# The fourth block's product ahead of the down chunk in the first pair of a chain, and the last norm from the accumulator, in a four-layer decoder trunk

## The chip, the cores and the metric

One NeuronCore of one Trainium2 chip runs the whole program. The metric is the device time of one execution in microseconds (us), given as the median of several runs; weights lie in HBM when it begins and are streamed in once. All arithmetic is float32. To get its precision from TensorE every weight chunk is split in two float32r parts (w_hi, w_lo), every activation likewise, and each product is made of three.

## What is computed

Four layers, each a half-step SwiGLU, an attention (stick-breaking, differential, forgetting, stick-breaking) and a second half-step SwiGLU, for 256 tokens of width 1024; at the end one more RMSNorm.

```python
D_MODEL, SEQ, DEPTH, D_FF, HEAD_DIM, EPS = 1024, 256, 4, 2816, 128, 1e-6

def rms_norm(x, g):
    y = x * rsqrt(mean(x * x, -1) + EPS)
    return y * g

def swiglu(x, w_gate, w_up, w_down):
    return (silu(x @ w_gate) * (x @ w_up)) @ w_down

for i in range(DEPTH):
    x = x + 0.5 * swiglu(rms_norm(x, norm_g[i, 0]), ffn_w_gate[i, 0], ffn_w_up[i, 0], ffn_w_down[i, 0])
    h = rms_norm(x, norm_g[i, 1])
    ...
    x = x + mix @ w_o[i]
    x = x + 0.5 * swiglu(rms_norm(x, norm_g[i, 2]), ffn_w_gate[i, 1], ffn_w_up[i, 1], ffn_w_down[i, 1])
return rms_norm(x, final_g)
```

## The kernel before

**Chunks.** The weights are worked through as 424 chunks of 128x2048 (1 MB each), in the order in which TensorE uses them. A DMA brings each into one of five slots of `raw` (or one of the two of `extra`), ScalarE copies it to `w_hi` (`hi`, L535), VectorE subtracts to `w_lo` (`lo`, L919), and TensorE multiplies; `w_hi` and `w_lo` are rings of six. `split_to(c)` on ScalarE and on VectorE takes all chunks up to c; where those calls stand among the other work sets the order of both engines. SP's queue issues the loads in the order of the list that `plan()` makes; each waits until its slot has been read (by `lo`, or by a form), and those behind it wait too.

**Units.** An FFN has 11 units of 256 hidden columns. A plain unit needs the chunks top and bottom (24 products of 128x512 each) and, when its hidden values are known, down (24 more, into the four banks of `acc`). Units 2 and 3, 4 and 5, 7 and 8, 9 and 10 are taken in pairs (`SEVEN` = 2, 4, 7, 9): a pair is a two by two block product (token halves by column blocks), made with seven products of 12 (`quarter`) in place of eight. Their chunks are b11, b21, b22 and the sums t1, t2, t3, t4. t1 is added up by DMAs (GpSimd's `first_weight_sums`); t3 = b22 + b12, t2 = t3 + b11 and t4 = b21 + t2 are *forms*, made by VectorE in place (`form`, L931, L935, L939). On the token side the sums are S1 to S4 (`token_sums_lo`, L1011). The four results are blocks c11, c21 (the first unit) and c12, c22 (the second): sums on VectorE (`sum_12` L1068, `sum_22` L1074), silu on ScalarE (c11 L618, c21 L623, c12 L629, c22 L636) and the gate product on VectorE (c11 L1078, c21 L1084, c12 L1090, c22 L1097). `pair_hidden` (L1687) transposes them on TensorE, `hidden_hi` (L558) and `hidden_lo` (L979) split them, and `unit_down` (L1493 to L1495 into acc) uses them.

**First and second of a chain.** Pair 4 follows pair 2, and 9 follows 7, with no plain unit between: 4 and 9 are *chained*. For a first pair (2 or 7) `pair_order` gives TensorE and the chunk list the order b11, t1, t2, b21, t3, down of the unit ahead, t4, b22. The transposes of its c11 and c21 stand behind the next pair's b11, and its own down chunk two products later. b11 of a t1 sum is loaded into slot `SUMS`, b22 into slot `EXTRA`, both of the tensor `extra`, which hold one pair at a time: b22 of a chained pair may be loaded when `lo` has taken b22 of the pair ahead of it.

**Around a norm.** `mean` (L961) is made by VectorE from sums of squares, GpSimd raises it to the power -1/2 (`r_col`, L499, L500). In the differential layer the last head pair's output product is kept apart (`output_apart`) and scaled afterwards: `mean_apart` (L1263), `r_apart` (L503, L504), `update` (L1385), with three `early_update`s (L1377) of the rest ahead of `mean_apart`; TensorE then turns x (L1537). At the end of the program ScalarE copies each bank of `acc`, which holds 2x, to x (`update`, L821), squares it (L830), and VectorE and ScalarE scale by `r_col` and `final_gain` (L1473, L1481, L890) into four stores.

## Time and profile before

| | us |
|---|---|
| median of 3 runs | 1882.12 (1881.24 to 1883.84) |
| the profiled execution | 1877.97 |
| its span, first to last instruction | 1876.2 |
| TensorE's products busy | 1853.3 (99%) |
| VectorE busy | 1562.6 (83%) |
| ScalarE busy | 1166.9 (62%) |
| granted clock of TensorE, mean | 0.999 |

Busy times are sums over instructions in one profiled execution. TensorE's products overlap each other in it, and their ends are modelled, so the idle time that the profile shows ahead of a product is less than the distance from start to start would give. The eight FFNs take about 177 us each, the four attentions about 110. All times of a row count from the start of the span.

### The profile page before, as it was taken

Reading aid. Unit: us, or ns where it says so; the run is one execution under the profiler, and the core shown is the slowest. Engines: PE = TensorE matmul, PEld = TensorE weight load, DVE = VectorE, ACT = ScalarE, POOL = GpSimd, SP = SyncE. Lnnn points to the kernel's source line nnn. Section 1 sums busy time; section 2 is a strip of 40 time slices with the busy share of each in tenths; the row PEclk is TensorE's granted clock in tenths of the full one; section 3 lists DMA queues with packets and bytes.
Section 4 is the critical chain, followed back from the end, with each engine's and each line's share of the span. In section 5 each row is a group of like instructions: output and inputs, shape, how many; then the busy total and the mean of one; then the engine's idle time right before and its main releaser. Section 6 shows DMA issues by size and latency. Waiting matters only on the chain.

```text
span 1876.2 us, 22732 instructions
## 1 busy us (share of the span) xinstructions
PE 1853.3 (99%) x9268; PEld 1566.1 (83%) x9268; DVE 1562.6 (83%) x1295; ACT 1166.9 (62%) x1220; POOL 60.3 (3%) x75
## 2 busy tenths in 40 slices
PE   9999999999999999999999999999999999999998
PEld 7788898888878899788888888987888888998886
DVE  7979568989888969998988995788898898569896
ACT  6666456666656645666665674465667567556665
POOL 1000000000000000100000000010000000001000
PEclk9999999999999999999999999999999999999999
DMA  8775445776677543577667763467775766437762
GB/s 300 261 290 226 180 157 180 226 289 264 200 249 272 235 151 134 183 254 286 266 187 272 255 247 121 149 227 245 270 278 190 274 221 246 157 108 252 277 238 79
DMA packets 59272, 417.28 MB, mean 222 GB/s; under 512 B 7192, under 2 KB 7456, under 8 KB 8992
## 3 DMA queue, kind: packets, MB, share of 16 engines
q1 hardware_dynamic: 53968, 380.09, 51.8%
q0 software_dynamic: 4608, 33.56, 9.5%
q10 hardware_dynamic: 592, 2.17, 0.3%
q8 instruction: 74, 1.21, 0.2%
q14 instruction: 30, 0.25, 0.0%
HBM read 414.74 MB, written 1.06 MB: 222 GB/s over the span
## 4 chain that ended last, share of the span: by engine, by line
PE 80%; DVE 12%; DMA 4%; ACT 2%; issue 2%; POOL 0%; SPq 0%; POOLq 0%; DVEq 0%; ACTq 0%
PE work L1493 16%; PE work L1495 16%; PE work L1494 16%; PE acc L1493 9%; PE acc L1495 9%; PE acc L1494 9%; DVE w_lo L919 6%; DMA extra<-stream_dram 3%; DMA raw<-stream_dram 1%; PE work L1687 1%; DVE raw L935 1%; PE acc L1537 1%; DVE raw L931 1%; PE work L1865 1%; PE work L1729 0%
## 5 line engine op out<-in xcount | busy, mean ns | idle before, releaser
L919 DVE TENSOR_TENSOR w_lo<-raw,w_hi 128x2048 fp32r<-128x2048 f32 x359 | 810.3, 2284 | 14.2 <-ACT w_hi L535 14.0
L535 ACT ACTIVATE w_hi<-raw 128x2048 fp32r<-128x2048 f32 x359 | 677.1, 1910 | 128.7 <-DVE raw L935 76.2
L1493 PE MATMUL work<-w_hi,xg 128*128 128x512 f32 x880 | 346.6, 394 | 1.1 <-DVE w_lo L919 1.1
L1495 PE MATMUL work<-w_hi,xg 128*128 128x512 f32 x880 | 343.5, 390 | 0.0
L1494 PE MATMUL work<-w_lo,xg 128*128 128x512 f32 x880 | 343.0, 390 | 0.0
L1493 PE MATMUL acc<-w_hi,m_hi 128*128 128x512 f32 x824 | 328.3, 398 | 6.3 <-DVE w_lo L919 6.1
L1495 PE MATMUL acc<-w_hi,m_lo 128*128 128x512 f32 x824 | 321.8, 391 | 0.0
L1494 PE MATMUL acc<-w_lo,m_hi 128*128 128x512 f32 x824 | 321.2, 390 | 0.0
L1495 PE MATMUL work<-w_hi,wide_r 128*128 128x512 f32 x512 | 199.8, 390 | 0.0
L1493 PEld LDWEIGHTS work<-w_hi,xg 128*128 128x128 f32 x880 | 165.4, 188 | 34.9 <-DVE w_lo L919 1.7
L1495 PEld LDWEIGHTS work<-w_hi,xg 128*128 128x128 f32 x880 | 165.3, 188 | 34.8
L1494 PEld LDWEIGHTS work<-w_lo,xg 128*128 128x128 f32 x880 | 165.5, 188 | 33.0
L1493 PEld LDWEIGHTS acc<-w_hi,m_hi 128*128 128x128 f32 x824 | 154.9, 188 | 38.1 <-DVE w_lo L919 8.4
L1495 PEld LDWEIGHTS acc<-w_hi,m_lo 128*128 128x128 f32 x824 | 154.7, 188 | 32.9
L1494 PEld LDWEIGHTS acc<-w_lo,m_hi 128*128 128x128 f32 x824 | 155.1, 188 | 30.0
L1493 PE MATMUL work<-xg,w_hi 128*128 128x256 f32 x512 | 148.9, 291 | 0.2
L919 DVE TENSOR_TENSOR w_lo<-extra,w_hi 128x2048 fp32r<-128x2048 f32 x64 | 146.2, 2284 | 0.0
L1494 PE MATMUL work<-xg,w_hi 128*128 128x256 f32 x512 | 145.0, 283 | 0.0
L1495 PE MATMUL work<-xg,w_lo 128*128 128x256 f32 x512 | 145.0, 283 | 0.0
L535 ACT ACTIVATE w_hi<-extra 128x2048 fp32r<-128x2048 f32 x64 | 122.3, 1911 | 4.4 <-DMA extra<-stream_dram 4.4
L1495 PEld LDWEIGHTS work<-w_hi,wide_r 128*128 128x128 f32 x512 | 96.1, 188 | 20.4
L1493 PE MATMUL work<-w_hi,scratch_r 128*128 128x512 f32 x256 | 103.1, 403 | 1.2 <-DVE w_lo L919 1.2
(211 smaller groups left out, 2324.8 us busy)
## 6 DMA issues: line engine op xcount, KB each, us to landing
raw<-stream_dram SPq DMA_DIRECT2D x295, 1024.0 KB, 7.3
extra<-stream_dram SPq DMA_DIRECT2D x64, 1024.0 KB, 4.9
extra<-stream_dram POOLq DMA_DIRECT2D x32, 1024.0 KB, 8.0
x<-x_dram SPq DMA_DIRECT2D x2, 512.0 KB, 8.2
raw<-stream_dram ACTq DMA_DIRECT2D x2, 512.0 KB, 8.0
scratch<-cum_rows ACTq DMA_DIRECT2D x1, 1024.0 KB, 6.5
cst<-consts_dram SPq DMA_DIRECT2D x1, 832.0 KB, 6.4
out_dram<-x SPq DMA_DIRECT2D x3, 256.0 KB, 2.5
```

Of the source, the lines that this page charges most:

```text
L535: nc.scalar.activation(w_hi[:, c % RING, :], raw_at(place), ACT.Copy).then_inc(hi_ready, 1)
L919: nc.vector.tensor_tensor(w_lo[:, c % RING, :], raw_at(place), w_hi[:, c % RING, :].bitcast(F32), ALU.subtract).then_inc(lo_ready, 1)
L931: ins = nc.vector.tensor_tensor(t3, b22, t3, ALU.add)
L935: ins = nc.vector.tensor_tensor(t2, t3, t2, ALU.add)
L1493: nc.tensor.matmul(dst, a_hi, b_hi, start=start, stop=False, skip_group_check=skip)
L1494: nc.tensor.matmul(dst, a_hi, b_lo, start=False, stop=False, skip_group_check=skip)
L1495: return nc.tensor.matmul(dst, a_lo, b_hi, start=False, stop=stop, skip_group_check=skip)
L1537: ins = nc.tensor.matmul(turned(bank)[:, d, :], x_part(bank)[:, d * P:(d + 1) * P], ident, is_transpose=True, start=d == 0, stop=d == FIRS ...
L1687: ins = nc.tensor.transpose(hidden_bank(s)[:, t * T + tb * P:t * T + (tb + 1) * P], h[:, t * P:(t + 1) * P], ident)
L1865: nc.tensor.matmul(bank, v[:, 0, cols], w[:, 0:T], start=True, stop=True)
```

## The change

Five pieces.

1. In a first pair b22's chunk and product stand ahead of the down chunk and of t4: b11, t1, t2, b21, t3, b22, down, t4 (`pair_order`, TensorE's `pair_step`).
2. The other engines follow: the blocks are now done in the order c11, c22, c12, c21 for every pair (`block_count`), with VectorE's sum and gate for c12 and ScalarE's silu for c12 earlier, and VectorE's forms of t3 and t2 of the chained pair behind gate c21.
3. `plan()` puts the load of a chained pair's b22 ahead of the load of its b21 (it was behind that of the down chunk). It still waits for `lo` of the b22 ahead.
4. From the second FFN on, `hidden_lo(0)` stands behind the third token sum's low part and the form of t3. At the end of the differential layer VectorE takes one more chunk's low part ahead of `mean_apart`, and the three early updates come behind it; ScalarE takes one chunk's high part earlier.
5. At the end of the program the four copies of `acc` to x are gone: squares, gains and outputs read `acc` itself, 2x, and the mean is taken with 4 EPS.

```diff
@@ pair_order
-    return [("b11", s), ("t1", s), ("t2", s), ("b21", s), ("t3", s), ("down", s - 1), ("t4", s), ("b22", s)]
+    return [("b11", s), ("t1", s), ("t2", s), ("b21", s), ("t3", s), ("b22", s), ("down", s - 1), ("t4", s)]
@@ plan
+            if what == "t4" and j in SEVEN[:-1] and not chained(following(j)):
+                loads.append(("b22", layer, n % 3, following(j), EXTRA, ("lo", c0 + order.index(("b22", j)) + 1)))
+            if what == "b21" and chained(j):
+                loads.append(("b22", layer, n % 3, j, EXTRA, ("lo", c0 + order.index(("b22", j - 2)) + 1)))
...
-            if what == "down" and chained(j + 2):
-                loads.append(("b22", layer, n % 3, j + 2, EXTRA, ("lo", c0 + order.index(("b22", j)) + 1)))
...
@@ ScalarE, pair_step
                     split_to(q + 8)
                     silu_22()
+                    split_to(q + 9)
+                    silu_12()
                     split_to(q + 10)
                     silu_21()
                     split_to(q + 11)
-                    silu_12()
@@ ScalarE, end of an attention
                     if j:
                         weights(b)
+                    if j == PAIRS and kind == DIFF:
+                        split_to(c0 + ATT_CHUNKS + 1)
@@ ScalarE, last norm
-                        update(n, i)
-                        square_sum(n, i)
+                        last_square_sum(i)
...
+            def last_square_sum(i):
+
+                n, bank = NORMS - 1, banks_of(NORMS - 1)[i]
+                act.wait_ge(acc_ready, BANKS * (n - 1) + i + 1)
+                act.wait_ge(squares_ready, BANKS * n + i - 1)
+                nc.scalar.activation(squares[i % 2], acc[:, bank, :], ACT.Square, scale=D ** -0.5,
                                      accum_out=sums[:, bank // TB, bank % TB:bank % TB + 1]).then_inc(squares_ready, 1)
@@ VectorE, plain_step
-                    if s == 1:
+                    if s == 1 and n:
+                        token_sums_lo((0, 1, 2))
+                    elif s == 1:
                         token_sums_lo((0, 1))
                         hidden_lo(0)
                         token_sums_lo((2,))
...
                     form("t3", q)
+                    if s == 1 and n:
+                        hidden_lo(0)
@@ VectorE, first_of_chain
                         if s == SEVEN[0]:
                             hidden_lo(s - 1)
-                        split_to(q + 5)
-                        if s == SEVEN[0]:
                             token_sums_lo((3,))
                         split_to(q + 6)
                         gate_11()
                         sum_22()
                         split_to(q + 7)
+                        sum_12()
                         split_to(q + 8)
                         gate_22()
-                        split_to(q + 9)
+                        gate_12()
+                        split_to(q + 10)
+                        gate_21()
                         form("t3", q + 8)
-                        gate_21()
-                        sum_12()
-                        split_to(q + 10)
                         form("t2", q + 8)
-                        gate_12()
                         hidden_lo(s)
@@ VectorE, end of the differential attention
                         apart_split(b)
+                        split_to(c0 + ATT_CHUNKS + 1)
+                        apart_mean()
                         for i in range(BANKS - 1):
                             early_update(i)
-                        apart_mean()
-                        split_to(c0 + ATT_CHUNKS + 1)
@@ VectorE, last norm
                     final_output(0, 0)
+                    final_mean(1)
                     final_gained()
-                    final_mean(1)
...
-                part = x_part(TB * half + tb)
-                nc.vector.scalar_tensor_tensor(out=part, in0=part, scalar=r_col[:, tb:tb + 1],
+                bank = TB * half + tb
+                nc.vector.scalar_tensor_tensor(out=x_part(bank), in0=acc[:, bank, :], scalar=r_col[:, tb:tb + 1],
@@ TensorE, pair_step of a first pair
                     quarter(chain, sum_of(S3), at["t3"], False, False)
+                    if s == SEVEN[0]:
+                        pe.wait_ge(token_lo_ready, BANKS * (f + 1))
+                    quarter(3, sum_of(S4), at["b22"], False, True)
                     unit_down(s - 1).then_inc(down_used, 1)
                     pe.wait_ge(pair_sums_ready, 2 * p + sum_count("c22"))
                     quarter(chain, block_of(1, 1), at["t4"], False, True)
-                    if s == SEVEN[0]:
-                        pe.wait_ge(token_lo_ready, BANKS * (f + 1))
-                    quarter(3, sum_of(S4), at["b22"], False, True)
```

What stands on VectorE in a row, in the first pair (unit 2) of the third FFN, before (line numbers of the kernel before; those of the changed kernel are 10 to 14 higher). `w_lo<-extra` is b22 where it follows the sum, and t1 where it precedes the form of t3 (L931):

```order
L1011 TENSOR_TENSOR wide_r<-wide,wide_r 128x512
L919 TENSOR_TENSOR w_lo<-raw,w_hi 128x2048
L1078 SCALAR_TENSOR_TENSOR scratch<-work,r_col,scratch 128x256
L1074 TENSOR_TENSOR scratch<-work,scratch 128x512
L919 TENSOR_TENSOR w_lo<-extra,w_hi 128x2048
L919 TENSOR_TENSOR w_lo<-raw,w_hi 128x2048
L1097 SCALAR_TENSOR_TENSOR scratch<-scratch,r_neg 128x256
L919 TENSOR_TENSOR w_lo<-extra,w_hi 128x2048
L931 TENSOR_TENSOR raw<-extra,raw 128x2048
L1084 SCALAR_TENSOR_TENSOR pair_h<-work,r_col,pair_h 128x256
L1068 TENSOR_TENSOR scratch<-work,scratch 128x512
L919 TENSOR_TENSOR w_lo<-raw,w_hi 128x2048
```

The same stretch of VectorE in the changed kernel:

```order
L1021 TENSOR_TENSOR wide_r<-wide,wide_r 128x512
L929 TENSOR_TENSOR w_lo<-extra,w_hi 128x2048
L929 TENSOR_TENSOR w_lo<-raw,w_hi 128x2048
L1092 SCALAR_TENSOR_TENSOR scratch<-work,r_col,scratch 128x256
L1088 TENSOR_TENSOR scratch<-work,scratch 128x512
L929 TENSOR_TENSOR w_lo<-raw,w_hi 128x2048
L1082 TENSOR_TENSOR scratch<-work,scratch 128x512
L929 TENSOR_TENSOR w_lo<-raw,w_hi 128x2048
L1111 SCALAR_TENSOR_TENSOR scratch<-scratch,r_neg 128x256
L1104 SCALAR_TENSOR_TENSOR scratch<-scratch,r_neg 128x256
L929 TENSOR_TENSOR w_lo<-extra,w_hi 128x2048
L929 TENSOR_TENSOR w_lo<-raw,w_hi 128x2048
```

b22's low part (the first `w_lo<-extra`) moved from behind the sum for c22 to the front, with the sum and the gate for c12 (L1082, L1104) up as well; gate c21 (L1098) and then the form of t3 follow behind the last row.

SP's queue around the loads of the chained pair 4 of the third FFN, before; `extra` alone is b11 for the sum t1 or b22, the rest goes to `raw`:

```order
L454 DMA raw<-stream_dram 128x2048 x8
L454 DMA extra<-stream_dram 128x2048
L454 DMA raw<-stream_dram 128x2048 x4
L454 DMA extra<-stream_dram 128x2048
L454 DMA raw<-stream_dram 128x2048
L454 DMA extra<-stream_dram 128x2048
```

And in the changed kernel:

```order
L454 DMA raw<-stream_dram 128x2048 x8
L454 DMA extra<-stream_dram 128x2048
L454 DMA raw<-stream_dram 128x2048 x2
L454 DMA extra<-stream_dram 128x2048
L454 DMA raw<-stream_dram 128x2048 x3
L454 DMA extra<-stream_dram 128x2048
```

The load of b22 (the second `extra`) went from behind b11, b12, b21 and down 2 to behind b11 and b12.

VectorE at the end of the differential layer, before:

```order
L919 TENSOR_TENSOR w_lo<-raw,w_hi 128x2048 x2
L1255 SCALAR_TENSOR_TENSOR m_lo<-work,subln_s,m_hi 128x256 x2
L1377 TENSOR_TENSOR x<-acc,x 128x512 x3
L1263 TENSOR_SCALAR mean_apart<-work 128x2
L919 TENSOR_TENSOR w_lo<-raw,w_hi 128x2048
L1385 SCALAR_TENSOR_TENSOR x<-work,r_apart,x 128x512 x2
```

And in the changed kernel:

```order
L929 TENSOR_TENSOR w_lo<-raw,w_hi 128x2048 x2
L1266 SCALAR_TENSOR_TENSOR m_lo<-work,subln_s,m_hi 128x256 x2
L929 TENSOR_TENSOR w_lo<-raw,w_hi 128x2048
L1274 TENSOR_SCALAR mean_apart<-work 128x2
L1388 TENSOR_TENSOR x<-acc,x 128x512 x3
L1396 SCALAR_TENSOR_TENSOR x<-work,r_apart,x 128x512 x2
```

The chunk's low part and the three early updates have changed places around `mean_apart`, for which GpSimd waits.

## Rows read from the trace of the kernel before

**Rows 1.** The page's first section: busy time, share of the span, instructions.

```profile
PE 1853.3 (99%) x9268; PEld 1566.1 (83%) x9268; DVE 1562.6 (83%) x1295; ACT 1166.9 (62%) x1220; POOL 60.3 (3%) x75
```

**Rows 2.** Timeline of TensorE, last FFN, start of down 2; start, length, engine, line.

```profile
1756.10 0.39 PE L1495 MATMUL work<-w_hi,xg 128*128 128x512 f32 x1
1756.33 0.60 PE L1687 MATMUL work<-cst,scratch 128*128 128x128 f32 x4
1756.68 0.48 PE L1493 MATMUL acc<-w_hi,m_hi 128*128 128x512 f32 x1
```

**Rows 3.** Waits of TensorE, 110 to 1870 us: total, times, longest.

```profile
PE acc L1493 <- DVE w_lo L919: 4.7, 5, 1.4
...
PE work L1687 <- DVE pair_h L1084: 0.4, 1, 0.4
```

**Rows 4.** Waits of TensorE, 60 to 90 us (first FFN).

```profile
PE work L1687 <- DVE pair_h L1084: 1.6, 1, 1.6
PE acc L1493 <- DVE w_lo L919: 1.4, 1, 1.4
```

**Rows 5.** Timeline of TensorE, third FFN, start of down 2.

```profile
542.09 0.60 PE L1687 MATMUL work<-cst,scratch 128*128 128x128 f32 x4
544.06 0.50 PE L1493 MATMUL acc<-w_hi,m_hi 128*128 128x512 f32 x1 [1.38 <-DVE w_lo L919]
```

**Rows 6.** Timeline of VectorE, third FFN, first pair; in brackets idle time and releaser.

```profile
519.03 2.29 DVE L919 TENSOR_TENSOR w_lo<-raw,w_hi 128x2048 fp32r<-128x2048 f32 x1 [0.35 <-ACT w_hi L535]
...
522.71 2.28 DVE L919 TENSOR_TENSOR w_lo<-extra,w_hi 128x2048 fp32r<-128x2048 f32 x1
...
533.12 2.29 DVE L931 TENSOR_TENSOR raw<-extra,raw 128x2048 f32<-128x2048 f32 x1 [3.33 <-DMA extra<-stream_dram]
...
541.72 4.49 DVE L919 TENSOR_TENSOR w_lo<-raw,w_hi 128x2048 fp32r<-128x2048 f32 x2
```

**Rows 7.** The loads of L454 issued from 514 to 531 us.

```profile
DMA to landing us min/median/max: 7.1/8.1/10.2
```

**Rows 8.** Windows: busy time of each engine, TensorE's clock, DMA share, GB/s.

```profile
530.00:535.00 5.00, 5.00 (x24) 4.15 (x23) 1.88 (x1) 2.28 (x2) 0.00 (x0) 1.00 0.99 359
```

**Rows 9.** Timeline of ScalarE, silu of c21 in the third FFN, unit 2.

```profile
530.19 0.47 ACT L623 ACTIVATE pair_h<-work,r_col 128x256 f32<-128x256 f32 x1 [2.57 <-PE work L1495]
```

**Rows 10.** Timeline of VectorE, first FFN, form of t3 for unit 4.

```profile
69.05 2.29 DVE L931 TENSOR_TENSOR raw<-extra,raw 128x2048 f32<-128x2048 f32 x1 [1.88 <-DMA extra<-stream_dram]
```

**Rows 11.** Timeline of VectorE, third FFN, low part of unit 0's h.

```profile
497.67 0.69 DVE L979 TENSOR_TENSOR m_lo<-work,m_hi 128x512 fp32r<-128x512 f32 x1 [2.97 <-ACT m_hi L558]
```

**Rows 12.** Timeline of VectorE, end of the differential layer.

```profile
758.96 1.87 DVE L1377 TENSOR_TENSOR x<-acc,x 128x512 f32<-128x512 f32 x3
761.63 0.16 DVE L1263 TENSOR_SCALAR mean_apart<-work 128x2 f32<-128x2 f32 x1 [0.80 <-PE work L1900]
761.71 2.28 DVE L919 TENSOR_TENSOR w_lo<-raw,w_hi 128x2048 fp32r<-128x2048 f32 x1
765.11 1.41 DVE L1385 SCALAR_TENSOR_TENSOR x<-work,r_apart,x 128x512 f32<-128x512 f32 x2 [1.12 <-POOL r_apart L504]
```

**Rows 13.** Timeline of GpSimd, the same place.

```profile
761.87 2.53 POOL L503 TENSOR_TENSOR r_apart<-mean_apart,half_neg 128x1 f32<-128x1 f32 x1 [97.48 <-DVE mean_apart L1263]
764.37 0.54 POOL L504 TENSOR_TENSOR r_apart<-mean_apart,half_neg 128x1 f32<-128x1 f32 x1
```

**Rows 14.** Timeline of GpSimd, end of the program.

```profile
1868.02 0.56 POOL L512 TENSOR_TENSOR r_col<-mean,half_neg 128x1 f32<-128x1 f32 x1 [63.73 <-DVE mean L1464]
1870.73 1.00 POOL L512 TENSOR_TENSOR r_col<-mean,half_neg 128x1 f32<-128x1 f32 x1 [2.15 <-DVE mean L1464]
```

**Rows 15.** Timeline of TensorE, first turn of x behind the differential layer.

```profile
765.92 0.55 PE L1537 MATMUL acc<-cst,x 128*128 128x128 f32 x3 [1.49 <-DVE x L1385]
```

**Rows 16.** Timeline of ScalarE, the last bank at the end of the program.

```profile
1869.11 0.60 ACT L821 ACTIVATE x<-acc 128x512 f32<-128x512 f32 x1
1869.74 0.63 ACT L830 ACTIVATE wide<-x 128x512 f32<-128x512 f32 x1
```

More of the change, by code:

```diff
@@ L85, in part_count, with block_count @@
     return [part for part, unit in pair_order(s) if unit == s].index(what) + 1
-def block_count(s, which):
-    return (("c11", "c22", "c12", "c21") if chained(s) else ("c11", "c22", "c21", "c12")).index(which) + 1
+def block_count(which):
+    return ("c11", "c22", "c12", "c21").index(which) + 1
 def sum_count(which):
@@ L184, in plan @@
                 loads.append((load, layer + 1, 0, SEVEN[0], place, ("lo", c0 + order.index((last, SEVEN[-1])) + 1)))
-            if what == "down" and chained(j + 2):
-                loads.append(("b22", layer, n % 3, j + 2, EXTRA, ("lo", c0 + order.index(("b22", j)) + 1)))
             if what == "down" and j + 1 in SEVEN[:-1]:
                 loads.append(("b11", layer, n % 3, following(j + 1), SUMS, ("lo", c0 + order.index(("t1", j + 1)) + 1)))
-            if what == "t4" and j in SEVEN[:-1] and not chained(following(j)):
-                loads.append(("b22", layer, n % 3, following(j), EXTRA, ("lo", c0 + order.index(("b22", j)) + 1)))
     return uses, loads
@@ L603, in seeded @@
                         if chained(s):
-                            act.wait_ge(pair_h_ready, 4 * (p - 1) + block_count(s - 2, "c21"))
+                            act.wait_ge(pair_h_ready, 4 * (p - 1) + block_count("c21"))
                         nc.scalar.activation(work[:, seed_bank(s), :], work[:, chain_bank(s), :],
@@ L830, in square_sum @@
                 nc.scalar.activation(squares[i % 2], x_part(bank), ACT.Square, scale=D ** -0.5,
+                                     accum_out=sums[:, bank // TB, bank % TB:bank % TB + 1]).then_inc(squares_ready, 1)
+            def last_square_sum(i):
[3 more added lines that the diff above has]
+                nc.scalar.activation(squares[i % 2], acc[:, bank, :], ACT.Square, scale=D ** -0.5,
                                      accum_out=sums[:, bank // TB, bank % TB:bank % TB + 1]).then_inc(squares_ready, 1)
@@ L1076, in gate_11 @@
                     def gate_11():
-                        dve.wait_ge(pair_silu_ready, 4 * p + block_count(s, "c11"))
+                        dve.wait_ge(pair_silu_ready, 4 * p + block_count("c11"))
                         nc.vector.scalar_tensor_tensor(out=first_part[:, 0:COLS], in0=work[:, seed_bank(s), COLS:2 * COLS],
@@ L1082, in gate_21 @@
                     def gate_21():
-                        dve.wait_ge(pair_silu_ready, 4 * p + block_count(s, "c21"))
+                        dve.wait_ge(pair_silu_ready, 4 * p + block_count("c21"))
                         nc.vector.scalar_tensor_tensor(out=pair_h[:], in0=work[:, chain_bank(s), COLS:2 * COLS],
@@ L1088, in gate_12 @@
                     def gate_12():
-                        dve.wait_ge(pair_silu_ready, 4 * p + block_count(s, "c12"))
+                        dve.wait_ge(pair_silu_ready, 4 * p + block_count("c12"))
                         nc.vector.scalar_tensor_tensor(out=first_sum[:, 0:COLS], in0=first_sum[:, COLS:2 * COLS],
@@ L1094, in gate_22 @@
                     def gate_22():
-                        dve.wait_ge(pair_silu_ready, 4 * p + block_count(s, "c22"))
+                        dve.wait_ge(pair_silu_ready, 4 * p + block_count("c22"))
                         place = fifth_copy(s)
@@ L1463, in final_mean @@
                 dve.wait_ge(squares_ready, BANKS * (NORMS - 1) + 2 * tb + 2)
-                nc.vector.scalar_tensor_tensor(out=mean[:, tb:tb + 1], in0=sums[:, 0, tb:tb + 1], scalar=EPS,
+                nc.vector.scalar_tensor_tensor(out=mean[:, tb:tb + 1], in0=sums[:, 0, tb:tb + 1], scalar=4 * EPS,
                                                in1=sums[:, 1, tb:tb + 1], op0=ALU.add,
@@ L1477, in final_gained @@
             def final_gained():
[L1479 removed]
+                dve.wait_ge(squares_ready, BANKS * NORMS)
                 dve.wait_ge(final_loaded, 16)
[L1481 removed]
+                nc.vector.tensor_tensor(last_gained, acc[:, 3, :], final_gain[:, HALF_D:], ALU.mult).then_inc(last_gained_ready, 1)
             dve.wait_ge(gain_loaded, 16)
@@ L1630, in pair_step @@
                     if chained(s):
-                        pe.wait_ge(pair_h_ready, 4 * (p - 1) + block_count(s - 2, "c11"))
+                        pe.wait_ge(pair_h_ready, 4 * (p - 1) + block_count("c11"))
                         quarter(chain, block_of(0, 0), at["b11"], True, False)
@@ L1682, in pair_hidden @@
                     for block in ("c12", "c22") if second else ("c11", "c21"):
-                        pe.wait_ge(pair_h_ready, 4 * p + block_count(first, block))
+                        pe.wait_ge(pair_h_ready, 4 * p + block_count(block))
                     for t in range(2):
@@ L1701, in plain_step @@
                         pe.wait_ge(lo_ready, c + 1)
-                        pe.wait_ge(pair_h_ready, 4 * p + block_count(s - 2, "c11"))
+                        pe.wait_ge(pair_h_ready, 4 * p + block_count("c11"))
                         gate_up(s, 0, c, top)
-                        pe.wait_ge(pair_h_ready, 4 * p + block_count(s - 2, "c21"))
+                        pe.wait_ge(pair_h_ready, 4 * p + block_count("c21"))
                         gate_up(s, 1, c, top).then_inc(top_used, 1)
```

2 lines of the change are left out of this document (removed).

## The prediction

> **What bounds the kernel now.** The page's first section comes first: TensorE has work for 1853.3 of 1876.2 us [rows 1], and its products follow each other every 0.23 us (1756.10 to 1756.33, [rows 2]). The change removes no product. So only two kinds of time can be won: gaps between products, and the ends. The view of TensorE's waits lists the gaps: from 110 us on five waits of a down product for VectorE's w_lo, 4.7 us in all, and one of 0.4 us for pair_h [rows 3]; one more of 1.5 us is for x, and comes in part 2; in the first FFN 1.6 us for pair_h and 1.4 us for w_lo [rows 4]. The idle time shown is less than the gap, because a product's modelled end overlaps the next one. With no wait a down product begins 0.35 us after the transposes ahead of it begin (1756.33 to 1756.68, [rows 2]); in the third FFN it is 1.97 us (542.09 to 544.06, [rows 5]), a gap of 1.62 where 1.38 is shown. I add 0.24 to each.
>
> Why is VectorE late there? Its timeline [rows 6] shows chunk after chunk, 2.20 us apart (two of 2.28 take 4.49 at 541.72), then 3.33 us idle ahead of the form of t3 for the second unit pair (533.12), released by the DMA into extra. Then 2.20 us steps again, so that the low part of down 2 is begun at 541.72 and done at 544.0, when the product of 544.06 begins. The load waited for is b22 of the next pair. It may overwrite extra only when VectorE has taken the low part of the present b22 (522.71 to 524.9); loads issued in this stretch take 7.1 to 10.2 us, median 8.1 [rows 7], with the DMA engines 0.99 busy [rows 8]: 525.0 plus 8.1 is 533.1. The cause is when the slot comes free.
>
> **Part 1, fourth block first.** In each of 16 first pairs (two for each of 8 FFNs) b22's product, its high and low parts and with them the release of extra go ahead of the down chunk and t4. No instruction is added or removed. In the third FFN I go along VectorE's new order with the old steps. The low part of the down chunk still begins at 519.03, since it waits for ScalarE's high part, which stands behind a copy of t2's sum. b22's low part lies ahead of it, so it ends by 519.0 instead of 524.9; with 8.1 us its load lands at 527, with the slowest of [rows 7] at 529.2. After 519.03: gate c11 and the sum for c22 as now, t4 at 522.7 to 524.9, the sum for c12 (0.6) to 525.5, b11 of the next pair to 527.7, two gates of 0.4 to 528.5, t1 and b21 to 532.9. Now gate c21 needs t4's product. Now TensorE is through with t4 at 530.0, and ScalarE begins its silu 0.2 us later and takes 0.47 (530.19, [rows 9]). With b22's 12 products (2.7 us) ahead of it t4 ends at 532.7: the silu runs from 532.9 to 533.4, the gate to 533.8. Then the forms of t3 and t2 (the load is there) to 538.2, a low part of h 0.6, and down 2's low part to 541.0, where it was 544.0. TensorE arrives: b11 (2.7) ends at 535.4, its transposes need c21, there since 533.8, **margin 1.6 us**; with 0.35, t1, b21 and 0.35 more it is at down 2 at 541.6, **margin 0.6 us**. Both gaps of this FFN close. The second first pair of each FFN (unit 7) has no gap now, and by the same steps gets none.
>
> The sum from 110 us on: 4.7 + 5 x 0.24 = 5.9, and 0.5 for the wait at 536 (0.36 idle there, and the overlap): **6.4 us**. The lower bound: the margin at down 2 is missed by 0.6 us in each of the five FFNs with such a wait, 3.0 us less: 3.4.
>
> In the first FFN VectorE waits 1.88 us for the same load (69.05, [rows 10]) and is behind from the start, so the gaps don't close: they move with its chain, which loses the 1.88 and gains about 0.1 of waiting for t4. The gap at the plain unit behind it hangs on loads issued behind the same chain and moves along. I take **1.8 us**; bounds 0.9 (b22 now stands behind a low part of the token sums, and TensorE can wait for it, up to half of the gain) and 3.3 (both waits of [rows 4] whole).
>
> Costed at nothing: from the second FFN on the first low part of h goes behind the third token sum and the form of t3, which is 0.6 + 2.2 = 2.8 us of work put into an idle time of 2.97 us (497.67, [rows 11]); if b12's load were late there, the first down product would wait behind the form. ScalarE's silu of c12 ahead of c21 stands while t4 is still running. On SP's queue b22's load now stands ahead of b21's and down 2's, and everything behind it waits for that release: b21's goes out by 519.4 instead of 515.7 and is needed as a low part at 530.7; down 2's goes out at 524.9 instead of 521.3 and is needed at 538.8. GpSimd's own loads (the adding ones) keep their release.
>
> **Part 2, end of the differential layer.** VectorE takes the next chunk's low part ahead of mean_apart, and three early updates behind it. mean_apart waited 0.8 us for TensorE's squares (761.63) anyway, so it starts as before. What follows differs: now a 2.28 us w_lo runs beside GpSimd's power (761.71, [rows 12]), which takes 2.53 us, and a second one 0.54 [rows 13]; with nothing beside it one takes 0.56 (1868.02, [rows 14]). x is ready for its update at 764.9, VectorE starts at 765.11, TensorE at 765.92 after 1.49 us idle [rows 15]. After the change three updates of 0.6 run there (to 763.5), with one operand in PSUM. No row shows a power beside such. Free it ends at 761.87 + 0.56 + 0.54 = 763.0, and the update starts when VectorE is through, 763.5: 1.5 us won. Held until 763.5 it ends at 764.5, the update begins at 764.6: 0.5 won. I take **1.5**, the row of 0.56 being nearest as long as one operand is not in SBUF; bounds 0.5 and 1.6.
>
> The Trainium skill, SBUF — State Buffer, Who interferes with whom, says that a VectorE instruction with two SBUF inputs blocks a GpSimd instruction that reads SBUF, one with at most one doesn't. By that rule, which the 2.53 beside a w_lo bears out, it is 1.5; were updates blocking too it would be 0.5.
>
> **Part 3, last norm from the accumulator.** Four copies of 0.6 leave ScalarE. Its last chain is a copy at 1869.11, which PSUM's last bank releases, and then the square at 1869.74 [rows 16]; without the copy the square starts 0.6 us sooner. A square out of PSUM has no row; a copy out of it took 0.60, the square 0.63 from SBUF, so 0.6 to 0.7. The last power (1.00 us, beside a VectorE step with two SBUF inputs, 1870.73, [rows 14]) may fall to 0.56, but VectorE then has the last three outputs to make in a row, as now. The end moves by **0.6 us**; bounds 0.3 and 0.9.
>
> **The sum.** 6.4 + 1.8 + 1.5 + 0.6 = 10.3 us. Against the profiled execution (1877.97 us, 1876.2 of it span) that is 1867.7. The three runs' median, 1882.12, lies 4.1 us above it; the same step gives **1871.8 us**. All lower bounds: 3.4 + 0.9 + 0.5 + 0.3 = 5.1, 1877.0. All upper ones: 6.7 + 3.3 + 1.6 + 0.9 = 12.5, 1869.6. Runs of one kernel differ by 2.6 us, so about 0.2% (3.8 us) can be told from no change.
>
> **Rivals.** *Down 2 stays late.* The idle time on VectorE goes, but its chain has only 0.6 us to spare; one more wait of 1.2 us, say for ScalarE, and each of five FFNs keeps 0.6: 7.3 us won, 1874.8. For: the margin; against: the last FFN, where VectorE has hardly a DMA wait and TensorE's product follows after 0.35 [rows 2].
>
> *The load in front only swaps places.* The DMA engines are 0.99 busy [rows 8], and b21's 1 MB now runs behind b22's. If it landed after 531 ScalarE's queue, and behind it silu c21, would be late; at 533 the gain of part 1 from 110 us on is gone and only 3.9 us are left: 1878.2, at the edge of no change. Against: by 519.4 plus 10.2 it lands by 529.6. The Trainium skill, DMA: Bandwidth & Descriptors, Two DMAs through the same engine are not ordered, says that in one queue of an engine descriptors start in order; by it b21's really stands behind, and the landing would be as I took it.
>
> *Slower: c21 ends last.* t4's form comes 2.7 us later on TensorE, and between it and the transposes of c11 and c21 stands one product of 2.7 us instead of two. The price starts when gate c21 is more than 1.6 us later than I reckon, at all 16 pairs, also at the eight of unit 7 that have no gap. At 2.6 us late: 16 x 1.0 lost, part 1 not won, parts 2 and 3 won: 1882.1 + 16 - 2.1 = 1896. Against: VectorE has nothing between b21's low part and the gate.
>
> *The change doesn't do what it says*: the release is not sooner because high parts are held by TensorE's progress. Then parts 2 and 3 alone are left, 2.1 us: 1880.0. Against: b22's high part needs only a ring place freed six chunks before.
>
> **Chances.** The forecast 0.58 (1869.6 to 1874); down 2 partly late 0.22; swapped places or no earlier release 0.12 (one half of it within 0.2%); c21 last, slower 0.05; more won than all upper bounds 0.03. The range 1868.5 to 1878 leaves out the slow case, half of the third, and little else. Faster by over 0.2% (below 1878.4) 0.86; within 0.2% 0.09; slower 0.05.
>
> **What the changed profile would show.** VectorE's form of t3 in unit 4 without a DMA wait in all eight FFNs; TensorE's waits from 110 us on without the w_lo row of a down product, and pair_h without waits; r_apart's first power near 0.6 us, x's wait under 0.3; ScalarE's last square ending near 0.8 us after TensorE's last product. Wrong would be: waits of TensorE for pair_h at many pairs, or of ScalarE for the DMA of b21 past 531 in the third FFN.

## The result, and the profile after

| | before | after |
|---|---|---|
| median (lowest to highest), runs side by side, us | 1881.24 (1874.98 to 1883.84), 5 runs | 1866.98 (1866.62 to 1867.86), 5 runs |
| the profiled execution, us | 1877.97 | 1866.62 |
| its span, us | 1876.2 | 1864.8 |

The ratio is 0.9926, with a 95% interval of 0.991 to 0.9942: 14.3 us less by the medians, 11.4 by the spans of the two profiles. The forecast was 10.3 for a profile, and 1871.8 us with 1868.5 to 1878.0 around it for the median. The direction and the change of the profile were foreseen; the time itself lies 1.5 us below the range.

Two more things stand in the table. Before's runs lie 8.9 us apart, those of the changed kernel 1.2. And before's median lies 3.3 us above its own profiled execution, after's 0.4. Both have the same cause, and the experiments found it.

The page of the changed kernel: the busy times, then the chain that ended last, by engine (TensorE's part of it was 80% before, VectorE's 12%).

```profile
PE 1851.8 (99%) x9268; PEld 1566.0 (84%) x9268; DVE 1562.9 (84%) x1295; ACT 1164.8 (62%) x1216; POOL 58.0 (3%) x75
...
PE 89%; DVE 5%; DMA 2%; ACT 1%; issue 1%; SPq 0%; DVEq 0%; ACTq 0%
```

TensorE's work is what it was [rows 1]; ScalarE has 1216 instructions, four less than before: the copies. TensorE's waits from 110 to 1870 us, which answer [rows 3] (total, times, longest), are these two and no other:

```profile
PE work L1504 <- DVE m_lo L1266: 0.5, 1, 0.5
PE work L1845 <- DVE k_t L1226: 0.3, 1, 0.3
```

The row of w_lo (4.7 us), the one of pair_h and the one of x are gone. VectorE in the third FFN, which answers [rows 6]; the brackets hold idle time and releaser:

```profile
512.24 2.28 DVE L929 TENSOR_TENSOR w_lo<-extra,w_hi 128x2048 fp32r<-128x2048 f32 x1
...
530.80 0.48 DVE L1098 SCALAR_TENSOR_TENSOR pair_h<-work,r_col,pair_h 128x256 f32<-128x256 f32 x1 [0.43 <-ACT pair_h L623]
531.21 2.28 DVE L941 TENSOR_TENSOR raw<-extra,raw 128x2048 f32<-128x2048 f32 x1
533.52 2.29 DVE L945 TENSOR_TENSOR raw<-raw 128x2048 f32<-128x2048 f32 x1
535.73 0.69 DVE L989 TENSOR_TENSOR m_lo<-work,m_hi 128x512 fp32r<-128x512 f32 x1
536.33 4.49 DVE L929 TENSOR_TENSOR w_lo<-raw,w_hi 128x2048 fp32r<-128x2048 f32 x2
```

b22's low part stands at 512.24, the gate of c21 at 530.80 with 0.43 us of waiting for its silu, and the form of t3 at 531.21 with no bracket: it waits for nothing. TensorE at the same place, transposes and then down 2, beside [rows 5]:

```profile
538.75 0.60 PE L1698 MATMUL work<-cst,scratch 128*128 128x128 f32 x4
539.11 0.47 PE L1504 MATMUL acc<-w_hi,m_hi 128*128 128x512 f32 x1
```

0.36 us from the one to the other, where it was 1.97. The end of the differential layer, GpSimd and then TensorE's first turn of x, beside [rows 13] and [rows 15]:

```profile
756.83 0.55 POOL L503 TENSOR_TENSOR r_apart<-mean_apart,half_neg 128x1 f32<-128x1 f32 x1 [97.45 <-DVE mean_apart L1274]
757.34 0.55 POOL L504 TENSOR_TENSOR r_apart<-mean_apart,half_neg 128x1 f32<-128x1 f32 x1
```

```profile
759.27 0.64 PE L1548 MATMUL acc<-cst,x 128*128 128x128 f32 x4
```

The first power takes 0.55 us where it took 2.53, and x's wait of 1.49 is gone.

**Where the 11.4 us went.** The same products are compared at their starts in the two profiles. Near 110 us, before and after:

```profile
111.47 0.27 PE L1687 MATMUL work<-cst,scratch 128*128 128x128 f32 x1
```

```profile
109.47 0.27 PE L1698 MATMUL work<-cst,scratch 128*128 128x128 f32 x1
```

| product | before | after | earlier by |
|---|---|---|---|
| transposes behind the first FFN's last pairs | 111.47 | 109.47 | 2.0 |
| third FFN, transposes ahead of down 2 | 542.09 | 538.75 | 3.3 |
| third FFN, down 2 | 544.06 | 539.11 | 5.0 |
| first turn of x behind the differential layer | 765.92 | 759.27 | 6.7 |
| last product | 1868.68 | 1857.83 | 10.9 |
| end of the span | 1876.2 | 1864.8 | 11.4 |

Of the 6.7 at x, 1.6 come between the power (761.87 before, 756.83 after: 5.0) and the turn of x. So the first FFN gave 2.0 (forecast 1.8), the pairs behind it 10.9 - 2.0 - 1.6 = 7.3 (6.4), the differential layer 1.6 (1.5), the end 0.5 (0.6).

In the first FFN the two gaps of [rows 4] have become smaller (0.2 and 0.7 us where they were 1.6 and 1.4), and a new one stands ahead of b22's product, which the forecast had named as possible:

```profile
56.92 0.47 PE L1504 MATMUL work<-w_hi,wide_r 128*128 128x512 f32 x1 [0.75 <-DVE w_lo L929]
```

### The profile page after: what moved, and what is told of

Read it like the earlier page. It is cut to its first block, busy times and chain, and to the rows that moved or that the text cites. A ratio compares the mean times of both kernels' runs of the same rounds, so it can differ in the third digit from the quotient of the medians.

```text
span 1864.8 us, 22728 instructions
## 1 busy us (share of the span) xinstructions
PE 1851.8 (99%) x9268; PEld 1566.0 (84%) x9268; DVE 1562.9 (84%) x1295; ACT 1164.8 (62%) x1216; POOL 58.0 (3%) x75
## 4 chain that ended last, share of the span: by engine, by line
PE 89%; DVE 5%; DMA 2%; ACT 1%; issue 1%; SPq 0%; DVEq 0%; ACTq 0%
PE work L1504 18%; PE work L1506 18%; PE work L1505 18%; PE acc L1506 10%; PE acc L1504 10%; PE acc L1505 10%; DVE w_lo L929 3%; DMA raw<-stream_dram 2%; PE work L1698 1%; PE acc L1548 1%; ACT w_hi L535 1%; PE work L1876 1%; PE work L1740 1%; PE work L1842 0%; PE work L1846 0%
```

## The experiments

They ask three things. First, which part brings what, and is the distance between before's median and its profile something that stays or something that the change removes? Second, if it is VectorE's wait for one load that makes TensorE's gaps, what closes them: the earlier release of extra, or the new order? Third, what are the small parts worth, and is anything left? Three theories run through the expectations. **A**: the gaps come from VectorE's wait for b22's load ahead of the form of t3, and the length of that load differs from execution to execution. **B**: the new order of products and low parts closes them whatever the load does. **C**: the early release is what counts. In the expectations of the next group "Rival B" is something else: before's median lies above its profile by an offset of the chip or the session that has nothing to do with the waits.

### One part at a time

The kernel before, unchanged, run once more:

> The kernel before, unchanged, profiled once more. The first profile (span 1876.2 us) was of an execution 4 us below the median of the runs. Theory A (TensorE's waits in this kernel hang on how long a load takes, and that differs from execution to execution): this profile shows waits for w_lo and pair_h that differ from the first by up to a few us, and the span goes with them; the runs spread over 3 us or more. Rival B (an offset of a chip or a session that has nothing to do with the waits): the waits are those of the first profile within 0.5 us in sum, whatever the span.

Part 1 alone (pieces 1 to 3 of the change, and nothing of pieces 4 and 5):

> Part 1 alone: fourth block first, with the order of ScalarE, VectorE and the loads that goes with it; without the moved low part of unit 0's h, without the change at the differential layer and in the last norm. Prediction's steps: 6.4 + 1.8 = 8.2 us off the span of the profiled execution of before (1868.0). Theory A: against the runs of before on the same chip about 12 us, with a spread of 1 us. Rival B: 8.2 us against them. In the profile: no wait of TensorE for w_lo of a down product from 110 us on; x still waits 1.5 us.

The end of the differential layer alone, on ScalarE and then on VectorE:

```diff
                     if j:
                         weights(b)
+                    if j == PAIRS and kind == DIFF:
+                        split_to(c0 + ATT_CHUNKS + 1)
...
                         apart_split(b)
+                        split_to(c0 + ATT_CHUNKS + 1)
+                        apart_mean()
                         for i in range(BANKS - 1):
                             early_update(i)
-                        apart_mean()
-                        split_to(c0 + ATT_CHUNKS + 1)
```

> The end of the differential layer alone: one low part ahead of mean_apart, the three early updates behind it, one high part earlier on ScalarE. Forecast: the first power of r_apart falls from 2.53 to 0.56 us, TensorE's wait for x from 1.5 us to under 0.3; 1.5 us in all, which the runs can't tell from no change. If an update with one operand in PSUM holds GpSimd as well, the power takes 1.7 us or more and 0.5 us are won. Theory A: spread and median of the runs otherwise as before.

The last norm from the accumulator alone:

> The last norm from the accumulator alone. Forecast: from the end of the last product to the end of the span 0.6 us less than in before (there 7.1 us), the last power 0.56 us in place of 1.00; in the runs no change that can be told.

| kernel | runs | median (lowest to highest), us | ratio to before (95%) | span of its profile |
|---|---|---|---|---|
| before, in the same session | 25 | 1879.62 (1874.05 to 1883.52) | | |
| before once more | 10 | 1880.13 (1877.21 to 1881.94) | 0.9999 (0.999 to 1.0008) | 1875.4 |
| part 1 | 4 | 1868.82 (1868.43 to 1869.23) | 0.9942 (0.9926 to 0.9959) | 1866.8 |
| differential layer | 10 | 1876.73 (1873.17 to 1881.68) | 0.9986 (0.9976 to 0.9997) | 1875.3 |
| last norm | 10 | 1877.83 (1874.59 to 1882.89) | 0.9997 (0.9985 to 1.001) | 1880.5 |

Part 1 by itself takes 10.8 us from the median, and the spread with it: 0.8 us between its runs, where the kernels without it have 4.7 to 9.5. Parts 2 and 3 are hardly told from nothing on that ground, though their profiles show them: with part 2 the first power takes 0.55 us and the wait for x is gone, with part 3 the span ends 7.0 us behind the start of the last product (1873.52 to 1880.5), where it was 7.5. What differs between executions is in the waits. VectorE's waits for this load from 110 to 1880 us, first before (TensorE's wait for w_lo beside it is in [rows 3], 4.7 us):

```profile
DVE raw L931 <- DMA extra<-stream_dram: 13.9, 9, 3.3
```

Before once more, TensorE's waits for w_lo and VectorE's for the load:

```profile
PE acc L1493 <- DVE w_lo L919: 4.4, 5, 1.3
...
DVE raw L931 <- DMA extra<-stream_dram: 12.6, 8, 2.6
```

The same two of the kernel with the last norm alone, whose profile is 4.3 us longer than before's:

```profile
PE acc L1500 <- DVE w_lo L926: 8.5, 7, 1.4
...
DVE raw L938 <- DMA extra<-stream_dram: 19.4, 9, 3.4
```

The last of these executions waited 5.5 us longer on VectorE than before's, 3.8 us longer on TensorE, and lasted 4.3 us longer in spite of its shorter end. Between the two executions of the kernel before the difference is small, 0.7 us in TensorE's waits for w_lo and pair_h and 0.8 in the span, so that pair alone would hardly decide against the offset; this third profile does. Which FFNs wait differs too, and at which pair: at unit 9 the form of t3 mostly waits 0.1 us, but 1.94 in the first FFN of before once more and 1.24 in the fourth of the kernel with the last norm alone. In the third one before has 3.33 us [rows 6]; in the other execution of the same kernel the form stands right behind the low part:

```profile
528.81 2.28 DVE L919 TENSOR_TENSOR w_lo<-extra,w_hi 128x2048 fp32r<-128x2048 f32 x1
531.14 2.29 DVE L931 TENSOR_TENSOR raw<-extra,raw 128x2048 f32<-128x2048 f32 x1
```

The loads around it say why: issues and landing times of before, 520 to 528 us, b22's issued at 525.0 and landing about 8 us later:

```profile
L454 SPq DMA_DIRECT2D extra<-stream_dram x1: 328/328/328, 525.0 to 525.0; - x1
...
DMA to landing us min/median/max: 7.1/8.0/10.2
```

The same loads in before once more; b22's is the shortest of the three, and was there when VectorE came:

```profile
L454 SPq DMA_DIRECT2D extra<-stream_dram x1: 328/328/328, 526.3 to 526.3; - x1
...
DMA to landing us min/median/max: 4.7/5.8/8.1
```

And the windows (the last two columns are the DMA engines' busy share and GB/s), first before, where the stretch of [rows 8] follows, then before once more:

```profile
520.00:525.00 5.00, 5.00 (x23) 4.13 (x22) 4.61 (x5) 5.00 (x5) 0.00 (x0) 1.00 0.92 354
525.00:530.00 5.00, 5.00 (x24) 4.14 (x23) 4.79 (x3) 2.13 (x2) 0.00 (x0) 1.00 0.98 356
```

```profile
520.00:525.00 5.00, 5.00 (x24) 4.14 (x23) 4.28 (x4) 5.00 (x6) 0.00 (x0) 1.00 1.01 403
525.00:530.00 5.00, 5.00 (x24) 4.14 (x23) 5.00 (x4) 3.32 (x2) 0.00 (x0) 1.00 0.96 370
530.00:535.00 5.00, 5.00 (x24) 4.14 (x23) 4.50 (x5) 2.28 (x2) 0.00 (x0) 1.00 1.02 416
```

At about the same busy share (0.92 to 0.99, and 0.96 to 1.02) the DMA engines moved 354 to 359 GB/s in the one execution and 370 to 416 in the other. The kernel before turned such differences into time, and the changed one doesn't.

The sessions of the experiments, each on another chip, differ in the same way: before's medians were 1879.62, 1881.54 and 1876.92 us in them, while the three kernels that have part 1's gain and nothing else (part 1 itself, and below the load made short and the form placed later) measured 1868.82, 1868.76 and 1868.6, one in each. So a chip or a session does have its part in before's median, but not as an offset outside the waits, as rival B had it: with the waits it goes.

### The load made short, with the old order

```diff
-                sp.dma_start(raw_at(place), stream[i]).then_inc(done[place] if place in done else raw_loaded[place], 16)
+                cols = CHUNK // 16 if LOADS[i][0] == "b22" and chained(LOADS[i][3]) else CHUNK
+                sp.dma_start(raw_at(place)[:, 0:cols], stream[i][:, 0:cols]).then_inc(
+                    done[place] if place in done else raw_loaded[place], 16)
```

> The kernel before, in which the load of a chained pair's b22 moves only the first 128 of its 2048 columns (the rest of that weight block is left out of the computation; every instruction of the engines stays). Nothing of the changed order is in it. Theory A (TensorE's gaps come from VectorE's wait for this load, and its length, 4.7 to 8.1 us in the profiles so far, differs from execution to execution): no form of t3 in unit 4 waits for a DMA, the gain of part 1 is there with the old order, 1868 to 1872 us, and the runs lie within 1 us of each other, where before's lie within 9. Rival B (the new order of products and low parts itself closes the gaps): 1876 to 1880 us, gaps and spread as before.

Measured: 1868.76 us (1868.59 to 1869.07, 4 runs), before beside it 1881.54 (1877.92 to 1885.56, 7 runs), ratio 0.993 (0.9914 to 0.9947). That is part 1's time and part 1's spread without anything of part 1. VectorE in the third FFN still waits a little, since the small load is queued behind others, but 0.72 us don't reach TensorE:

```profile
524.30 2.28 DVE L921 TENSOR_TENSOR w_lo<-extra,w_hi 128x2048 fp32r<-128x2048 f32 x1
527.30 2.29 DVE L933 TENSOR_TENSOR raw<-extra,raw 128x2048 f32<-128x2048 f32 x1 [0.72 <-DMA extra<-stream_dram]
```

Theory B falls as far as it says that the new order is needed; A stands. One thing is left open here: the edit also takes 16 times 15/16 of a megabyte off the DMA engines, which may make other loads shorter. The form placed later, below, gets the same time with every load whole.

### The new order with the old release, and later ones

The changed kernel, with b22's load behind down 2's again and waiting for a later low part:

```diff
-            if what == "b21" and chained(j):
-                loads.append(("b22", layer, n % 3, j, EXTRA, ("lo", c0 + order.index(("b22", j - 2)) + 1)))
...
+            if what == "down" and chained(j + 2):
+                loads.append(("b22", layer, n % 3, j + 2, EXTRA, ("lo", c0 + order.index(("t4", j)) + 1)))
```

> The changed kernel, but b22's load of a chained pair stands behind down 2's load again and may go when VectorE has taken t4's low part (522.4 us in the third FFN of the changed kernel, where b22's is through at 514.5), so nearly as late as before. The form of t3 is due at 531.2. Theory A, taken with its numbers: 522.4 plus 4.7 to 8.1 is 527 to 530.5, no wait outside the first FFN, 1867 to 1868.5 us. Rival C (it is the early release that closes the gaps): half of the gain or more is lost, 1873 us or more.

The next has `("b11", j + 2)` there:

> The same, with the release by the low part of the next pair's b11 (525.2 us in the third FFN). Theory A: landing at 529.9 to 533.3, waits of 0 to 2.1 us ahead of the form; TensorE notices what is over 0.8 us (down 2's low part ends 0.8 us ahead of its first use), so 0 to 1.3 us in each of eight FFNs: 1868 to 1874 us, and runs that differ by more than 1 us. Rival B: 1867 us, no effect.

And the third `("t1", j + 2)`:

> The same, with the release by the low part of the next pair's t1 (528.2 us in the third FFN). Theory A: landing at 532.9 to 536.3, waits of 1.7 to 5.1 us, of which TensorE notices all but 0.8: 0.9 to 4.3 us in each of eight FFNs, 1874 to 1901 us, near 1888, slower than the kernel before, and the order of everything on VectorE and TensorE is still the new one. Rival B: 1867 us.

| release by the low part of | in the third FFN issued at | median (lowest to highest), 4 runs, us | ratio (95%) |
|---|---|---|---|
| b22 (the change, session of the result) | 514.5 | 1866.98 (1866.62 to 1867.86), 5 runs | 0.9926 (0.991 to 0.9942) |
| t4 | 522.5 | 1866.61 (1866.36 to 1868.28) | 0.9921 (0.9903 to 0.9938) |
| b11 | 525.1 | 1866.79 (1866.52 to 1867.2) | 0.992 (0.9903 to 0.9937) |
| t1 | 535.4, 7 us of it the delay of this kernel up to there | 1892.42 (1891.55 to 1893.95) | 1.0054 (1.0034 to 1.0075) |

Ten microseconds of earlier release are worth nothing, and then one step later costs 25.6. C falls: the piece of the change that puts the load in front isn't needed. For b11 my numbers said that some executions would wait, 1868 to 1874 us, and that was a miss: all four runs lie between 1866.52 and 1867.2, and in the one that was profiled no form waits for b22's load. In its third FFN the load issued at 525.1 took 5.9 us, and the form of t3 found it by a hair:

```profile
L454 SPq DMA_DIRECT2D extra<-stream_dram x2: 328/328/328, 525.1 to 528.1; - x2
...
DMA to landing us min/median/max: 5.9/6.9/7.9
```

```profile
531.10 2.29 DVE L941 TENSOR_TENSOR raw<-extra,raw 128x2048 f32<-128x2048 f32 x1
```

With the release by t1 it waits, and TensorE waits behind it; first VectorE in the third FFN, then the waits of TensorE and of VectorE, 110 us to the end:

```profile
540.31 2.29 DVE L941 TENSOR_TENSOR raw<-extra,raw 128x2048 f32<-128x2048 f32 x1 [1.78 <-DMA extra<-stream_dram]
```

```profile
PE acc L1504 <- DVE w_lo L929: 18.7, 15, 1.4
...
DVE raw L941 <- DMA extra<-stream_dram: 27.3, 15, 2.0
```

Fifteen waits of 1.8 us on VectorE give fifteen of 1.25 on TensorE; 25.6 us over 16 pairs are 1.6 each (the sixteenth, 2.3 us on VectorE, lies in the first FFN, before 110 us). The expectation took 0.8 of a wait to be hidden, from the end of the low part to the product that first reads w_lo. But TensorE waits for the low part ahead of down 2's first product, and to there the changed kernel has 0.5 us (538.6 to 539.11). By the medians 0.2 is hidden; where the other 0.3 goes I haven't followed. This release also shows that both chained pairs of an FFN hang on this load, unit 9 as well as unit 4. So B falls at this end too: with the whole new order in place the kernel is slower than before when the load comes late.

### The form placed later, and nothing else

What release and order have in common is when VectorE comes to the form. In the old order of products, this edit alone puts one low part and one gate ahead of it:

```diff
                         split_to(q + 9)
-                        form("t3", q + 8)
+                        split_to(q + 10)
                         gate_21()
+                        form("t3", q + 8)
                         sum_12()
-                        split_to(q + 10)
                         form("t2", q + 8)
```

> The kernel before with one edit on VectorE: in the chained pair the low part of b21 and gate c21 go ahead of the form of t3, the sum for c12 behind it. Products, loads and releases are before's. In the third FFN b21's low part then runs from 529.8 to 532.0, the gate to 532.4, the form of t3 begins between 532.4 and 533.1 (landing), forms and sum end by 538.1, gate, low part of h and down 2's low part by 541.3, where it is 544.0 now and is first used at about 542.4. If it is only the place where VectorE meets the load that matters: most of part 1's gain with the old order of products, 1868 to 1873 us. If the new order of products is needed: 1877 us or more.

Measured: 1868.6 us (1868.12 to 1869.35, 4 runs) beside 1876.92 for before (1874.23 to 1879.06, 9 runs), ratio 0.9958 (0.9945 to 0.9972). VectorE in the third FFN:

```profile
526.44 2.28 DVE L919 TENSOR_TENSOR w_lo<-raw,w_hi 128x2048 fp32r<-128x2048 f32 x1
528.64 0.47 DVE L1084 SCALAR_TENSOR_TENSOR pair_h<-work,r_col,pair_h 128x256 f32<-128x256 f32 x1
529.03 2.28 DVE L931 TENSOR_TENSOR raw<-extra,raw 128x2048 f32<-128x2048 f32 x1
```

No wait here, and the time of part 1 (1868.82) with before's products, loads and releases. From 110 us on the form waits for this load twice, in the sixth and the seventh FFN:

```profile
DVE raw L931 <- DMA extra<-stream_dram: 0.5, 2, 0.4
```

TensorE has no wait for w_lo from 110 us on: in the third FFN down 2's low part ends 1.1 us ahead of down 2 (537.3 to 538.45), 0.5 in the changed kernel. The load needs no help: the other work that VectorE has to do before down 2 has only to be done while it runs.

### The small parts, and a better version

> The changed kernel with the last norm as before. Against the changed kernel's 1867.0: part 3 by the forecast is worth 0.6 us (0.3 to 0.9), so 1867.3 to 1867.9; if the copies were hidden anyway 1867.0.

> The changed kernel with hidden_lo(0) back between the second and the third token sum's low part in every FFN. The forecast costed the move at nothing: 1867.0, within 0.3 us. If the move is part of the gain: 1867.5 or more.

The last one is the changed kernel with one number changed:

```diff
-EARLY_LOADS = 20
+EARLY_LOADS = 30
```

> The changed kernel with EARLY_LOADS 30 in place of 20: the five small loads of constants on SP's queue, issued from 86.2 to 88.8 us, go out ten chunks later. The load behind them, issued at 88.86, is the one for which ScalarE waits 6.49 us at 95.65, and TensorE at about 101. If the issue time counts, that load goes 2.6 us sooner and TensorE's gap of about 1 us in the first FFN goes: 1866.0 to 1866.6 us; if the DMA engines are the limit there, 1867.0.

| kernel, all in one session | runs | median (lowest to highest), us |
|---|---|---|
| changed, last norm as before | 5 | 1867.30 (1867.14 to 1868.79) |
| changed, hidden_lo(0) where it was | 4 | 1866.96 (1866.47 to 1867.89) |
| changed, constants later | 5 | 1865.78 (1865.02 to 1866.15) |

The move of hidden_lo(0) is worth nothing that can be told. The last norm is worth 0.3 us by these medians, too little for so few runs; the profiles show 0.5. The last product and the end of the span are 1868.68 and 1876.2 before, 1857.83 and 1864.8 after, 7.5 and 7.0 us apart. The constants give 1.2 us against the kernel without the hidden_lo move, more than the 0.4 to 1.0 that I expected: all five runs lie below all others here. Against before the ratio is 0.9942 (0.993 to 0.9955), in a session in which before's median was 1876.92. In the changed kernel, on ScalarE:

```profile
95.65 1.92 ACT L535 ACTIVATE w_hi<-raw 128x2048 fp32r<-128x2048 f32 x1 [6.49 <-DMA raw<-stream_dram]
```

And with the constants later; five small DMAs no longer stand ahead of this chunk's load in SP's queue:

```profile
93.22 1.92 ACT L535 ACTIVATE w_hi<-raw 128x2048 fp32r<-128x2048 f32 x1 [3.90 <-DMA raw<-stream_dram]
```

TensorE's wait of 0.8 us at 101 us is gone with it. This kernel beats before, and by 1.2 us (0.06%) the changed one too (1866.62 to 1867.86 in the session of the result; the two never ran in one session).

## Why the time was missed and the mechanism was not

**What bounds the kernel, and the third FFN: right.** The walk put the transposes of c21 1.6 us behind the gate and down 2 0.6 us behind its low part. Measured: the gate's successor starts at 531.21 and the transposes of c11 and c21 at 532.8, 1.6 us; the low part of down 2 ends at 538.6 and down 2 starts at 539.11, 0.5 us. Every sign that was named appeared: no DMA wait at the form of t3 in unit 4 in any of the eight FFNs, no w_lo wait from 110 us on, no pair_h, the first power at 0.55. In the first FFN the walk was right in size (2.0 for 1.8) but not in its picture: the gaps there didn't only move, they shrank, and a wait of 0.75 us ahead of b22's product took part of it back.

**The cause of the wait: right, but only half of the remedy.** "The cause is when the slot comes free" is true of the kernel before, given where the form stands. The walk itself moved the form 4 us later as well, and the runs show that this alone does it; with the form there, the slot may come free 10 us later than in the change.

**The sum for a profile: 10.3 forecast, 11.4 measured.** The terms were 6.4 + 1.8 + 1.5 + 0.6, measured 7.3 + 2.0 + 1.6 + 0.5. The first one is low by 0.9: it adds up the waits that the view lists and one estimate of 0.24 for each, and short gaps that a modelled end covers are in no list. The largest of them is down 2 of the fourth FFN before, 0.69 us behind its transposes where 0.35 is a start without a wait, with no bracket:

```profile
830.69 0.60 PE L1687 MATMUL work<-cst,scratch 128*128 128x128 f32 x4
831.38 0.51 PE L1493 MATMUL acc<-w_hi,m_hi 128*128 128x512 f32 x1
```

The other 0.6 lies in starts that are each 0.1 us late or less, or isn't followed; the distance of the same product in two profiles counts them all. The upper bound of this term, 6.7, stands in the prediction's sum without a working, and 7.3 lies above it.

**The failed step** is "The three runs' median, 1882.12, lies 4.1 us above it; the same step gives 1871.8 us." It takes the distance of the median from the profiled execution as something that lies outside the kernel's waits and stays. It is made of those waits. One profile shows one draw of sixteen load times, two in each FFN, and before's 56 runs of all sessions reach from 1874.05 to 1885.56 us, with medians from 1876.92 to 1881.54; the draw in the profile was a mild one. Once VectorE no longer meets the load, what differs between draws goes as well: after's median lies 0.4 us above its profile, that of part 1 0.2. Without the step the time would have been 1867.7, within 0.7 us. The range was drawn by the same step, so its low end, 1868.5, stood above that number.

The rows could have told. Three median runs of 1881 to 1884 beside a profile of 1878 showed that executions of this kernel differ by more than 0.2%, and [rows 7] showed loads from 7.1 to 10.2 us on which the waits hang. A load whose length differs and that releases the critical chain is a source of such spread, and a change that takes it off the chain takes the spread.

**The rivals.** "Down 2 stays late" didn't come. "The load in front only swaps places" didn't either, but its half, that the earlier load isn't what helps, is true by the releases. "c21 ends last" didn't come; its margin was 1.6 us as reckoned. That a miss is paid at all 16 pairs, as this rival reckoned, the release by t1 shows, though there it is the form and not the gate that comes late: 1.6 us at each, 25.6 us in all. "The change doesn't do what it says" didn't come either: b22's load went out at 514.5 in the third FFN, where it was 525.0.

**The powers.** At the end of the differential layer the taken value, 1.5, was right: beside three updates that read acc in PSUM the power takes 0.55. At the end of the program it fell from 1.00 [rows 14], beside a step that read x and the gain from SBUF, to 0.55 beside one that reads acc from PSUM and the gain, VectorE and then GpSimd:

```profile
1859.06 0.69 DVE L1492 TENSOR_TENSOR wide<-acc,extra 128x512 f32<-128x512 f32 x1
```

```profile
1859.22 0.55 POOL L512 TENSOR_TENSOR r_col<-mean,half_neg 128x1 f32<-128x1 f32 x1 [2.15 <-DVE mean L1475]
```

The Trainium skill, SBUF — State Buffer, Who interferes with whom, gives this (two SBUF inputs on VectorE block GpSimd's reads, one does not); both pairs of rows agree.

## What to carry to other kernels

A profile is one execution. If the critical chain waits for a load whose length differs between executions, the profile's wait is one draw, and the distance between the profile and the median is part of what a change of that wait wins: don't carry it over to the new time. When an engine waits for a transfer ahead of work that isn't urgent, first look for independent work behind it that can go in front; here two moved calls on VectorE, the form and one low part, gave what part 1 gave with its reordering of products, chunks and loads on four engines.

## What the hardware showed that was not expected

- The DMA engines at a busy share of 0.92 to 1.02 moved 354 to 359 GB/s in one execution and 370 to 416 in another of the same kernel, in the same stretch; a 1 MB load took 8 us in the one and 4.7 in the other. What sets the rate in an execution isn't known; no run varied it.
- Nothing is lost smoothly: a release 10.6 us later cost nothing, the next one in the program's order 25.6 us (1.4%).
